# Per-head sums of squares as 32-column products into one PSUM bank, one logarithm and one exponential for four heads, roots spread to all partitions by transfers

## The reference, cut to what matters

```python
def l2_norm(x):                      # queries and keys of the gated delta rule, 4 heads of 128
    return xf * lax.rsqrt(jnp.sum(xf * xf, axis=-1, keepdims=True) + EPS)
def rms_norm(x, g):                  # q, k and index key of the sparse attention; output of the delta rule
    y = xf * lax.rsqrt(jnp.mean(xf * xf, axis=-1, keepdims=True) + EPS)
...
q = l2_norm(q.reshape(Bsz, T, A_HEADS, A_DK)) * (A_DK ** -0.5)
k = l2_norm(k.reshape(Bsz, T, A_HEADS, A_DK))
o = rms_norm(o, norm_g) * jax.nn.silu(z...)
...
q = rms_norm_2(heads(q), q_gain)     # second block, even layer: 8 heads of 64, q and k
var = jnp.mean(jnp.square(o - mu), axis=-1, keepdims=True)   # odd layer: 4 heads of 512
o = (o - mu) * lax.rsqrt(var + EPS) * gn_gain
```

## Time and profile before

| | |
|---|---|
| median of 3 runs | 1572.06 us (1569.5 to 1572.73) |
| span of the profiled execution | 1571.2 us |
| PE busy | 1558.9 us (99%) |
| DVE busy | 1155.8 us (74%) |
| ACT busy | 885.8 us (56%) |
| POOL busy | 53.2 us (3%) |
| moved by DMA | 262.98 MB, 167 GB/s |

### The profile page before, as it was taken

One profiled execution on the slowest core, in us unless ns is written; L12 is line 12 of the kernel. 1 busy time (PEld: TensorE's weight loads), 2 busy tenths in 40 slices (PEclk: granted clock), 3 DMA queues, 4 the chain that ended last, 5 costly groups with the idle time before them and its releaser, 6 DMA issues.

```text
span 1571.2 us, 34539 instructions
## 1 busy us (share of the span) xinstructions
PE 1558.9 (99%) x12620; PEld 1527.2 (97%) x12620; DVE 1155.8 (74%) x1911; ACT 885.8 (56%) x1388; POOL 53.2 (3%) x44
## 2 busy tenths in 40 slices
PE   8999999999999999999999999999999999999999
PEld 8999899999999998999999999999999999999999
DVE  7789787766568798787765768888756757678864
ACT  5665656555455755665554565666545456566652
POOL 0101001000000010010000000000010000100000
PEclk9999999999999999999999999999999999999999
DMA  6753154655546442447666546466565545656663
GB/s 216 228 154 112 55 188 148 193 175 174 175 148 187 147 120 82 151 147 239 195 185 188 173 130 188 148 201 187 181 188 182 167 140 161 187 158 191 187 192 130
DMA packets 274350, 262.98 MB, mean 167 GB/s; under 512 B 20337, under 2 KB 272785, under 8 KB 274257
## 3 DMA queue, kind: packets, MB, share of 16 engines
q1 hardware_dynamic: 272960, 257.67, 53.0%
q0 software_dynamic: 1008, 3.97, 0.8%
q10 hardware_dynamic: 288, 0.07, 0.0%
HBM read 256.91 MB, written 3.43 MB: 166 GB/s over the span
## 4 chain that ended last, share of the span: by engine, by line
PE 84%; DVE 9%; ACT 3%; issue 2%; DMA 2%; SPq 0%; DVEq 0%; ACTq 0%
PE lin L552 23%; PE lin L555 23%; PE lin L560 23%; PE aux L895 6%; PE lin L895 3%; DVE wL L539 3%; PE lin L606 2%; DMA stage<-in_w_in 1%; PE lin L577 1%; PE lin L641 1%; DVE cT L2045 1%; DVE nT L2501 1%; ACT wH L530 1%; DVE nL L2506 1%; PE aux L555 1%
## 5 line engine op out<-in xcount | busy, mean ns | idle before, releaser
L530 ACT ACTIVATE wH<-stage 128x1024 fp32r<-128x1024 f32 x488 | 494.2, 1049 | 461.4 <-PE lin L555 321.2
L539 DVE TENSOR_TENSOR wL<-stage,wH 128x1024 fp32r<-128x1024 f32 x488 | 571.1, 1213 | 129.9 <-PE lin L560 69.0
L552 PE MATMUL lin<-nH,wH 128*128 128x256 f32 (+2 forms) x2256 | 558.2, 286 | 0.6 <-DVE u L2550 0.3
L555 PE MATMUL lin<-nL,wH 128*128 128x256 f32 (+2 forms) x2256 | 553.5, 284 | 0.0
L552 PEld LDWEIGHTS lin<-nH,wH 128*128 128x128 f32 x2256 | 424.6, 188 | 4.0 <-issue 2.4
L555 PEld LDWEIGHTS lin<-nL,wH 128*128 128x128 f32 x2256 | 425.9, 189 | 0.9 <-issue 0.7
L560 PE MATMUL lin<-nH,wL 128*128 128x256 f32 (+2 forms) x2256 | 295.0, 283 | 0.0
L560 PEld LDWEIGHTS lin<-nH,wL 128*128 128x128 f32 x2256 | 281.4, 188 | 0.1
L552 PE MATMUL lin<-aH,wH 128*128 128x256 f32 (+1 forms) x704 | 172.3, 284 | 0.0
L555 PE MATMUL lin<-aL,wH 128*128 128x256 f32 (+1 forms) x704 | 172.2, 284 | 0.0
L555 PEld LDWEIGHTS lin<-aL,wH 128*128 128x128 f32 x704 | 132.9, 189 | 0.0
(11 more groups left out here) (392 smaller groups left out, 2092.0 us busy)
## 6 DMA issues: line engine op xcount, KB each, us to landing
stage<-in_w_up SPq DMA_DIRECT2D x88, 512.0 KB, 4.6
stage<-in_ffn_w_up SPq DMA_DIRECT2D x88, 512.0 KB, 4.3
stage<-in_w_in SPq DMA_DIRECT2D x52, 512.0 KB, 5.0
stage<-in_w_down SPq DMA_DIRECT2D x40, 512.0 KB, 3.7
stage<-in_ffn_w_down SPq DMA_DIRECT2D x40, 512.0 KB, 4.2
stage<-in_w_gate SPq DMA_DIRECT2D x32, 512.0 KB, 4.6
stage<-in_even_w_in SPq DMA_DIRECT2D x24, 512.0 KB, 4.5
stage<-in_w_out SPq DMA_DIRECT2D x16, 512.0 KB, 4.4
```

Of the source, the lines that this page charges most:

```text
L530: nc.scalar.activation(wH[:, s, ks, 0:n], stage[:, s, ks, 0:n], ACT.Copy).then_inc(sem["whi"], 1)
L539: nc.vector.tensor_tensor(wL[:, s, ks, 0:n], stage[:, s, ks, 0:n], wH[:, s, ks, 0:n].bitcast(F32), ALU.subtract).then_inc(sem["wlo"], 1)
L552: mm = nc.tensor.matmul(banks[b][0:rows_, 0:width], wH[:, s, k, cols], xh, start=start and n == 0, stop=False)
L555: mm = nc.tensor.matmul(banks[b][0:rows_, 0:width], wH[:, s, k, cols], xl, start=False, stop=False)
```

## The change

For each group of four heads (`ssq`, `ssk`, `sbq`, `so`, `eq`, `ow`) the four products take only 32 columns of ones each, and each writes 32 partitions of one common bank: head h to partitions 32h to 32h+31. ACT makes one logarithm and one exponential over `[128, T]` into a tile of one row per partition (`root_q`, `root_k`, `root_late`, `roots_e`, `roots_w`). The factor of head h is then in partitions 32h to 32h+31 alone, and POOL issues a transfer per head (`heads_out`) that copies the row of partition 32h to all 128 partitions of `rnq`, `rnk`, `rnb`, `rno` or `rn4`; for `eq` there are eight, each to 64 partitions of `rne`. DVE waits for all transfers of a group. `sbk` and `sik` stay as they were.

```diff
+            def heads_out(to, rows_, counter, n, landed):
+                pool.wait_ge(sem[counter], n)
+                for h in range(4):
+                    pool.dma_start(to[:, h, :].unsqueeze(1), rows_[32 * h:32 * h + 1, :].unsqueeze(1).to_broadcast([1, P, to.shape[2]])).then_inc(sem[landed], 16)
...
                 for n, (kind, x) in enumerate((("i", rawT[:, 20:24, META:T]), ("i", ikr[:, :].unsqueeze(1)), ...
+                    if n == 1:
+                        heads_out(rnq, root_q, "roots", at("roots", l, 1), "roots_q")
+                        heads_out(rnk, root_k, "roots", at("roots", l, 2), "roots_k")
+                    if n == 2:
+                        heads_out(rnb[:, 0:4], root_late, "roots", at("roots", l, 3), "roots_b")
...
+                heads_out(rno, root_late, "roots", at("roots", l, 4), "roots_o")
...
+            pool.wait_ge(sem["eroots"], 1)
+            for c in range(4):
+                for p0 in (0, HALF):
+                    row = 32 * c + p0 // 4
+                    pool.dma_start(rne[p0:p0 + HALF, 2 * c:2 * c + 2, :]..., roots_e[row:row + 1, :]....to_broadcast([1, HALF, 512])).then_inc(sem["eroots_in"], 16)
...
+            heads_out(rn4, roots_w, "oroots", 1, "oroots_in")
...
-                def head_squares(h0):
-                    for h in range(h0, h0 + 4):
-                        name = f"ss{'qk'[h // 4]}{h % 4}"
-                        mm(begin(name, l)[:, 0:T], ones, sqh[:, h, :]).then_inc(filled(name), 1)
+                def head_squares(name, x):
+                    ps = begin(name, l)
+                    for h in range(4):
+                        t = mm(ps[32 * h:32 * h + 32, 0:T], ones[:, 0:32], x[:, h, :])
+                    t.then_inc(filled(name), 1)
...
-                root_log([f"ssq{h}" for h in range(4)], rnq, 1.0)
+                root_log(["ssq"], root_q[:, :].unsqueeze(1), 1.0)
+                root("ssq", root_q[:, :], lnq_col, "roots")
...
-                root_log(["ssk0"], rnk, 1.0)
+                root_log(["ssk"], root_k[:, :].unsqueeze(1), 1.0)
+                root("ssk", root_k[:, :], 0.0, "roots")
...
-                root_log([f"ssk{h}" for h in range(1, 4)], rnk, 1.0, 1)
                 root_log(["sik"], rni, 1.0 / P)
-                root("ssq3", rnq, lnq_col)
-                root("ssk3", rnk, 0.0)
...
-                dve.wait_ge(sem["rn"], at("rn", l, 1))
+                dve.wait_ge(sem["roots_q"], at("roots_q", l, 64))
                 v.tensor_tensor(cT[:, 0:4, :], cT[:, 0:4, :], rnq[:, :, :], ALU.mult).then_inc(sem["qk_unit"], 1)
-                dve.wait_ge(sem["rn"], at("rn", l, 2))
+                dve.wait_ge(sem["roots_k"], at("roots_k", l, 64))
...
+                dve.wait_ge(sem["roots_b"], at("roots_b", l, 64))
                 v.scalar_tensor_tensor(rawT[:, 16:20, :], ..., rnb[:, 0:4, :], ...)
...
+                dve.wait_ge(sem["roots_o"], at("roots_o", l, 64))
                 for h in range(4):
-                    dve.wait_ge(sem["rno"], at("rno", l, h + 1))
...
-                dve.wait_ge(sem["ern"], n + 1)
+                dve.wait_ge(sem["eroots_in"], 8 * 16)
...
-                dve.wait_ge(sem["ovar"], h + 1)
+                dve.wait_ge(sem["oroots_in"], 4 * 16)
```

More of the change, by code:

```diff
@@ L184 @@
 JOBS = (
-    ["ms1"] + [f"ssq{h}" for h in range(4)] + ["ta"] + [f"ssk{h}" for h in range(4)] + ["sik", "gc", "tv"]
+    ["ms1", "ssq", "ta", "ssk", "sik", "gc", "tv"]
     + ["gb0", "gb1"] + ["kk0", "qk0", "kk1", "qk1"] + ["gb2", "kk2", "qk2"]
     + [f"ix0{e}" for e in range(2)] + [f"ix1{e}" for e in range(4)]
-    + [f"sbq{h}" for h in range(4)] + ["sbk"] + ["Y1_4", "Y2_4"] + [x for b in range(3) for x in (f"kt{b}", f"vt{b}")]
+    + ["sbq", "sbk"] + ["Y1_4", "Y2_4"] + [x for b in range(3) for x in (f"kt{b}", f"vt{b}")]
     + ["X1_4", "X2_4", "Y1_5", "T1_5", "Y2_5", "T2_5", "X1_5", "X2_5", "Y1_6", "T1_6", "Y2_6", "T2_6", "vn0", "s0"]
@@ L191 @@
     + [f"s{h}2" for h in "abcd"] + ["o1", "dS1", "pv1", "kS2"] + [f"pt{b}_2" for b in range(3)] + ["vn2", "pv2", "o2"]
-    + [f"so{h}" for h in range(4)] + [("loop", 2, [f"br{b}" for b in range(4)])] + ["ms2"]
+    + ["so"] + [("loop", 2, [f"br{b}" for b in range(4)])] + ["ms2"]
 )
@@ L201 @@
 JOBS2 = (
-    ["ems"] + [f"eq{c}" for c in range(4)] + ["e00", "e01"] + [f"e1{e}" for e in range(4)] + [f"et0{g}" for g in range(2)]
+    ["ems", "eq", "e00", "e01"] + [f"e1{e}" for e in range(4)] + [f"et0{g}" for g in range(2)]
     + [f"et1{g}{b}" for g in range(2) for b in range(2)] + ["ev0", "ev1", "emf", "oms"]
     + [f"os{h}" for h in range(4)] + [f"oo{h}{e}" for h in range(4) for e in range(2)]
-    + [f"ow{h}" for h in range(4)] + ["omf"]
+    + ["ow", "omf"]
 )
@@ L213 @@
     "sq": DC, "rstd": 2, "n": 2 * DC, "nh": DC, "nl": DC,
[L214 removed]
+    "conv": 12, "silu": 3, "sq_heads": 2, "sq_att": 1, "sq_ik": 1, "rn": 2, "roots": 4, "roots_q": 4 * 16, "roots_k": 4 * 16, "roots_b": 4 * 16, "roots_o": 4 * 16, "qk_unit": 2, "att_unit": 3,
     "sp_in": 1, "sp_ln": 1, "gt": 4, "eg": 4, "dec": 3, "kdx": 1, "qe": 1,
     "rates_out": 3 * 16, "rates_in": 3 * 16, "rates_exp": 1, "rope_cos": 4, "rope_sin": 4, "swapped": 2 * 4 * 16, "rope": 4, "score": 6, "ml": 2 * len(UPPER), "mt_out": 3 * 16, "mt_in": 3 * 16, "solved": 1, "bt_out": 2 * 16, "b_out": 3 * 16, "x_back": 2 * 16, "a_back": 3 * 16,
[L217 removed]
+    "nmx": 3, "soft": 2, "pn": 3, "ob_h": 3, "sqo": 3, "oa": 4, "oa_h": 4, "oa_l": 4,
     "gates": 12, "y": 8, "yh": 4, "yl": 4,
@@ L965, in turned @@
                     t.then_inc(filled(name), 1)
-                head_squares(0)
+                head_squares("ssq", sqh[:, 0:4])
                 turned("ta", iab, IDX_DIM, 16, (sem["iab"], at("iab", l, 1)))
-                head_squares(4)
+                head_squares("ssk", sqh[:, 4:8])
                 pe.wait_ge(sem["sq_ik"], at("sq_ik", l, 1))
@@ L1061, in layer @@
                 pe.wait_ge(sem["sq_att"], at("sq_att", l, 1))
-                for h, name in enumerate([f"sbq{h}" for h in range(4)] + ["sbk"]):
-                    mm(begin(name, l)[:, 0:T], ones, sq_att[:, h, :]).then_inc(filled(name), 1)
+                head_squares("sbq", sq_att[:, 0:4])
+                mm(begin("sbk", l)[:, 0:T], ones, sq_att[:, 4, :]).then_inc(filled("sbk"), 1)
                 below(4)
@@ L1187, in layer @@
                 pe.wait_ge(sem["sqo"], at("sqo", l, 3))
-                for h in range(4):
-                    mm(begin(f"so{h}", l)[:, 0:T], ones, sqo[:, h, :]).then_inc(filled(f"so{h}"), 1)
+                head_squares("so", sqo)
                 gate(3, [1])
@@ L1400, in _ @@
             odd_g(0, 1)
+            pe.wait_ge(sem["osum"], 2)
+            ps = begin("ow", L)
             for h in range(4):
-                pe.wait_ge(sem["osum"], h // 2 + 1)
-                mm(begin(f"ow{h}", L)[:, 0:SEQ], ones, sq16[:, 4 * h, :]).then_inc(filled(f"ow{h}"), 1)
+                t = mm(ps[32 * h:32 * h + 32, 0:SEQ], ones[:, 0:32], sq16[:, 4 * h, :])
+            t.then_inc(filled("ow"), 1)
             for i in range(1, 4):
@@ L1630, in layer @@
                 gate_hi(0, [1])
-                root_log([f"sbq{h}" for h in range(4)] + ["sbk"], rnb, 1.0 / P)
-                root("sbk", rnb, 0.0)
+                root_log(["sbq"], root_late[:, :].unsqueeze(1), 1.0 / P)
+                root("sbq", root_late[:, :], 0.0, "roots")
+                root_log(["sbk"], rnb, 1.0 / P, 4)
+                root("sbk", rnb[:, 4, :], 0.0)
                 below(4)
@@ L1695, in layer @@
                 weighted_values(2)
[L1696 to L1701, removed]
+                root_log(["so"], root_late[:, :].unsqueeze(1), 1.0 / P)
+                root("so", root_late[:, :], 0.0, "roots")
                 for h in range(4):
@@ L1848, in _ @@
             take(M_E + 2, 0, lambda c: ght[:, c, :].unsqueeze(1))
[L1849 to L1855, removed]
+            act.wait_ge(*full("eq", L))
+            f(roots_e, bank("eq")[:, :], Ln, bias=eps_col, scale=1.0 / 64).then_inc(emptied("eq"), 1)
+            act.wait_ge(*read("eq", L))
+            f(roots_e, roots_e, Exp, scale=-0.5).then_inc(sem["eroots"], 1)
             take(M_E + 2, 1, lambda c: ght[:, 2 + c, :].unsqueeze(1))
@@ L1931, in _ @@
             act.preload_act_table_set(EXP_LN)
[L1932 to L1937, removed]
+            act.wait_ge(*full("ow", L))
+            f(roots_w, bank("ow")[:, 0:SEQ], Ln, bias=eps_col, scale=1.0 / 512).then_inc(emptied("ow"), 1)
+            act.wait_ge(*read("ow", L))
+            f(roots_w, roots_w, Exp, scale=-0.5).then_inc(sem["oroots"], 1)
             act.preload_act_table_set(SILU)
```

25 lines of the change are left out of this document (17 added, 8 removed).

## The result

| | before | after |
|---|---|---|
| median of the runs | 1570.10 us (1569.5 to 1572.73, 5 runs) | 1708.98 us (1704.94 to 1710.0, 5 runs) |
| span of the profiled execution | 1571.2 us | 1708.2 us |
| PE busy | 1558.9 us | 1566.8 us |
| PE not busy (span less busy) | 12.3 us | 141.4 us |

The ratio is 1.0872 (95% interval 1.086 to 1.0884): slower by 137.0 us of span. The prediction said 1704 us, 1575 to 1810.

A forecast was written before the change was run, and what follows sets the result against it. PE was taken to bound the kernel, level with DVE in some stretches. Waits for the roots (88 + 20 + 8) and slow clock (16) add 132 us to 1571.2, giving 1703, stated as 1704 us; range 1575 to 1810.

The forecast's parts named there:

- PE's part: Squares on PE: four 32-column products run at once, a group falls from 1.8 to 0.8 us, in all 11 us of PE time.
- the free case: Rival: the spread costs nothing, a group lands 4 us after its exponential; 1564 to 1571 us, 1568 likeliest; chance 0.16.
- The transfers: POOL's spread of roots from one partition: 15 us a group of 272, 14 for ow, 28 for eq, each plus 1.8 fixed.
- The nearest row, iq_s: Profile row of transfers reading a quarter of the partitions, 154 GB/s; taken as reason to lean to the upper bound.
- My upper bound: Transfers: the source serves one engine at a time at 20.7 GB/s, 6.7 us a transfer, 27 us a group.
- The estimate that the prediction drew from the Trainium skill: Transfers limited by ports of 27.2 GB/s: 5.1 us each, 10 to 20 us a group, time 1640 to 1745 us.
- Who waits: Waits for late roots: 44 us a layer (ssq and ssk 20, sbq 12, so 12), 88 in all; eq 20, ow 8.
- The clock: Granted clock under 1 after each of the eight new waits, 2 us each: 16 us.
- The sum: Waits of 88, 20 and 8 plus clock 16 make 132 us on the profile's 1571.2.
- Wholly in turn: Rival: transfers served one after another, 27 us a group and 50 for eq; 1833 us; chance 0.08.

The follow-up runs named there:

- e4: Changed kernel without its transfers of roots; DVE multiplies each partition by the root row standing in it (wrong heads): 1565.97 us, 0.9964 of the kernel before.
- e1: Changed kernel, but each transfer reads the 32 equal rows of its head (16 rows for rne) instead of one: 1584.94 us, 1.0087 of the kernel before.
- e3: Changed kernel, but each transfer reads two rows 16 apart, 32h and 32h+16, rne as it was: 1652.38 us, 1.0518 of the kernel before.
- e5: Changed kernel, still one source row per transfer, but row 40h instead of 32h, for all groups but rne: 1642.21 us, 1.0450 of the kernel before.
- e6: Changed kernel with all transfers issued, but nobody waits for them at ssq, ssk and sbq; those of ssq and ssk go to DRAM: 1695.85 us.
- e8: Kernel before with only ssq, ssk and sbq changed, their transfers reading the 32 rows of a head: 1574.05 us, 1.0022 of the kernel before.

## Why the prediction held, step by step

- **PE's part: right.** 0.67 us for the eight passes where 0.85 was said; four quarters work at once. With the change of the array's division a group costs 0.7 us where 0.8 was said (from the first of sq_att's squares, 147.72, to the product behind them, 148.88, less 0.46 for `sbk`). By e4 the rest of the free case (1564 to 1571) is right as well, at 1565.97. Missed: that PE, freed at ssq and ssk, would stand and then run at half clock. I had put its gain there at 0.1 to 0.3 us and priced no clock in the free case.
- **The transfers: the right side, and a mean of two errors.** Said: 15 us for a group of 272, 14 for ow, 28 for eq, each plus 1.8. Measured: so 20.6 from issue to DVE, that is 18.8; ow 18.2 less 1.8, 16.4; eq 18.0 less 1.8, 16.2. The groups of one row per head were 2 to 4 us dearer, eq 12 cheaper. The nearest row, iq_s, told the direction. My upper bound was built on one engine's rate; what e1, e3 and e5 show is a limit of the source's place, shared by sixteen engines at once, which would let rne's rows 16 apart count for two, as they do in e3. The estimate that the prediction drew from the Trainium skill, 5.1 us a transfer, was nearer (18.8 / 4 = 4.7).
- **Who waits.** sbq was said to cost 12 us a layer and cost some 15, so 12 and 17, eq 20 and 10.7, ow 8 and 10.7: in each the difference goes the way of the landing and is within 3 us of it. For ssq and ssk 20 was said and PE stood some 23, 20 of them behind the transfers. But the step that I gave for it, DVE's wait for `rnq` and `rnk`, is only one of two that ended within 3 us of each other. The text put what the spread does to other transfers at nothing; e6 shows that at ssq and ssk it is enough by itself. That the number came out right there is luck: both delays last as long as the same packets.
- **The clock.** Half clock behind each wait: 16 us were put down for eight waits. PE was busy 7.9 us longer with some 11 us less work: 19. The trace agrees: in the stretches at a granted clock of 0.50 PE was busy for 47.7 us, against 6.5 before, and half of the difference is 20.6.
- **The sum.** 132 against 137. Terms that were off by 3 to 9 us had both signs; the total is better than its parts.
- **The rivals.** "Wholly in turn" (1833) came by the rate of one engine and fell with it, although the transfers do go largely in turn: rno's four landed 7.2, 11.3, 15.9 and 18.9 us behind their issues. The free case is e4's, and needs a spread that takes nothing from anyone.

## What to carry to other kernels

Before a row is spread by DMA, ask from how many places the source is read: transfers from one partition each gave 30 GB/s with every engine occupied, 32 partitions that held the same values anyway brought 124 of the 137 us back. Price such a transfer not only by its own landing but by what other queues want to move meanwhile; the small, late-looking transfer in front of a solver may be the one that pays. And time taken off PE in front of a wait that another engine ends is not gained, and can be lost twice by the clock; put other work in front of the wait first, then look in the chain for what sets the stage.

## What I had not expected of the hardware

- SP's issue of three transfers of 2 KB and less took 21.6 us while POOL's broadcast packets were under way, against 1.1 us before: a full set of engines holds up the issuing queue, not just the landing.
- Changing a source row's number from 32h to 40h took 67 us off a kernel.
- In e4 a wait of PE of 1.28 us and one of 1.82, with 1 us of small products between them, were followed by 6 us at a granted clock of 0.50; in e8 and in the changed kernel much the same waits were followed by 3.4 us.
